# Merge products as three passes over high and low parts, with outgoing weights parted one unit ahead

## Chip, cores and metric

One core of a Trainium2 chip. The time is that of one execution on the device in microseconds. TensorE (PE) does the matrix products, VectorE (DVE), ScalarE (ACT) and GpSimd (POOL) the elementwise work, and SyncE (SP) issues most DMAs. The profile's weight loads stand under PEld.

## What is computed

A decoder trunk of two layers over 512 tokens of width 1024. Each layer normalizes x, projects it, runs four mixers and merges them with sigmoid gates; an output projection and an MLP follow:

```python
h = rms_norm(x, mix_norm_g)
p_gdn, p_mla, p_rwkv, p_dsa, gates = split(h @ w_in)   # gates: four of width 1024
y_b = mixer_b(p_b)                                     # (512, 256) for each branch b
merged = sum over b of sigmoid(gate_b) * (y_b @ w_out_b)
x = x + merged @ w_o
x = x + relu(rms_norm(x) @ w_up) ** 2 @ w_down
```

The mixers are a gated DeltaNet (GDN), multi-head latent attention (MLA), RWKV-7 and an attention over the 128 keys that an indexer selects for each query (DSA). The change touches `y_b @ w_out_b` alone.

## The kernel before

**Units.** All large weights come in one stream of 134 units a layer, a unit being 1024 rows by 128 columns, in the order of `UNITS` (L59 to 77). 32 of a layer's units are `("merge", branch, i)`: the gate weights for output columns 128i to 128i+127 and, with them, the outgoing weights `w_out` of the same columns (256 rows). The branches come in the order RWKV (2), GDN (0), MLA (1), DSA (3). In this text merges are numbered 0 to 31 in a layer: 0 to 7 RWKV, 8 to 15 GDN, 16 to 23 MLA, 24 to 31 DSA.

**Large products in parts.** A gate or projection is not an fp32 product. The weights are split into `w_hi` (an ACT copy to fp32r, L1179) and `w_lo` (what is left, a POOL subtraction in two halves, L447); the activations likewise into `h_hi` and `h_lo`. `split_product` (L480) makes 24 passes: `w_hi` by `h_hi` and by `h_lo` for eight tiles of rows, then `w_lo` by `h_hi`. `SPLIT = 2` split units exist at once; ACT makes the next one in `split_next` (L1173) when it has taken the result of the unit two before. SP loads unit g when POOL is done with unit g-3 (`RING = 3`, L409).

**Merges.** `merge` (L549) makes two gates and then two outgoing products (`merge_outputs`, L556). An outgoing product is a plain fp32 one over two tiles of 128 rows: `out_ring` (the weights, six slots) by `yo` (the mixer's output, two buffers in turn). ACT takes each gate through a sigmoid into `sg` (`merge_sig`, L1142), DVE multiplies it with the outgoing product and adds it to `mg` (`merge`, L1675) and signals `mg_done`. SP loads the outgoing weights right behind the gate weights of the same unit and waits for `mg_done` of the merge six before (L414).

**Order of the work.** Each engine runs a written-out list; an instruction that waits holds up all behind it on its engine. In a layer: RWKV's projections and scan; merges 0 to 3, whose products wait for `r_out`; GDN's preparation, merges 4 to 7, GDN's scan; DSA's projections; merges 8 to 15, between them index scores on PE (`index_pair`), ACT (`rectify_pair`) and DVE (`score_pair`), and on DVE the selection of 128 keys, dealt out in steps by `go_on` (L2002), each a MAX8 and a MATCH_REPLACE. Then MLA's attention with the gates of merges 16 to 18 made in pieces between its products, the gate of 19, and the products of 16 to 19 once `m_y` counts 8, that is once all outputs are evicted; merges 20 to 23; DSA's attention with 24 to 26 in pieces, 27, products, 28 to 31; then `wo`, `up` and `down`.

**DVE around MLA's attention** (L2069 to 2078): `attention`, `go_on(9)`, four merges, `go_on(8)`, two merges, the rest of the selection, two merges, DSA's `attention`. DVE's `attention` (L1692) takes scores from `bank_v` (L1706) and scales the exponentials (L1714, L1715). ACT's `attention` (L1213) makes the exponentials, evicts the transposes and evicts each output block of 128x128 to `yo` (L1232), the last of them three steps after its last exponential. `R["o"]` times `R["g"]` (L1887) and `G["o"]` times `G["z"]` (L1938) are the outputs of the other two mixers, written to `yo` by DVE.

## Time and profile before

| | us |
|---|---|
| median of 3 runs | 2047.19 (2046.12 to 2048.41) |
| profiled execution | 2048.0 |
| its span, first to last instruction | 2046.2 |

| engine | busy | share of the span |
|---|---|---|
| PE | 1988.9 | 97% |
| PEld | 1527.7 | 75% |
| DVE | 1090.5 | 53% |
| ACT | 768.6 | 38% |
| POOL | 737.9 | 36% |

Busy time is what lies between start and end of instructions. Each instruction's line is that of `kernel.py`; where a helper issues it (L1513 is `tt`, L1516 `ts`), tile names tell which it is. An idle time in brackets behind an instruction names what ended it. Matmul durations overlap (0.39 us each at a spacing of 0.23), so the sums of PE are read in the chain of waits, where pieces follow each other without overlap.

### The profile page before, as it was taken

The page shows a single profiled execution, that of the slowest core. Times are in us where ns is not written, and L with a number is a line of the kernel's source. Part 1 is how long each engine was busy: PE and PEld are TensorE (multiplying, and loading weights), DVE is VectorE, ACT ScalarE, POOL GpSimd, SP SyncE. Part 2 cuts the span into 40 slices and gives each one's busy share as a digit, 9 for nine tenths or more (in the row PEclk, how much of TensorE's full clock was granted, in tenths as well). Part 3 has the DMA queues.
Part 4 walks back from the last instruction along what each step waited for, and adds up shares of the span by engine and source line. Part 5 has one row for each costly group of instructions (what it writes and reads, how often), then busy time and mean ns, then how long its engine had stood idle before and what let it go on. Part 6 is the DMA issues. An engine that isn't in the chain of part 4 may idle for free.

```text
span 2046.2 us, 31754 instructions
## 1 busy us (share of the span) xinstructions
PE 1988.9 (97%) x13120; PEld 1527.7 (75%) x13120; DVE 1090.5 (53%) x1816; ACT 768.6 (38%) x1207; POOL 737.9 (36%) x551
## 2 busy tenths in 40 slices
PE   6999999999999999999999999999999999999997
PEld 4778787756667888888877877776566778888886
DVE  8785555896833422222387756379966343222223
ACT  4542523344353342322354353234344434332323
POOL 3431313422323444444445132243213344444442
PEclk9999999999999999999999999999999999999999
DMA  6220212221312333232232111123122223333232
GB/s 234 74 77 27 65 33 67 83 75 50 121 49 83 112 96 100 93 103 93 93 124 86 52 37 58 43 78 101 52 71 87 67 83 103 93 98 99 93 103 73
DMA packets 51807, 170.21 MB, mean 83 GB/s; under 512 B 5696, under 2 KB 14016, under 8 KB 51024
## 3 DMA queue, kind: packets, MB, share of 16 engines
q1 hardware_dynamic: 50448, 163.11, 24.9%
q0 software_dynamic: 1216, 5.07, 0.7%
q8 instruction: 105, 1.72, 0.3%
q14 instruction: 38, 0.31, 0.0%
HBM read 160.82 MB, written 7.34 MB: 82 GB/s over the span
## 4 chain that ended last, share of the span: by engine, by line
PE 84%; DVE 11%; ACT 3%; issue 1%; DMA 0%; POOL 0%; ACTq 0%; SPq 0%; DVEq 0%
PE bank_a L486 13%; PE bank_a L492 13%; PE bank_a L487 12%; PE bank_v L492 7%; PE bank_v L486 7%; PE bank_v L487 7%; PE bank_v L562 4%; PE bank_v L640 3%; DVE arena L1513 1%; PE bank_a L799 1%; PE bank_f L594 1%; PE bank_f L600 1%; PE bank_f L573 1%; DVE mg L1519 1%; PE bank_a L788 1%
## 5 line engine op out<-in xcount | busy, mean ns | idle before, releaser
L447 POOL TENSOR_TENSOR w_lo<-ring,w_hi 128x512 fp32r<-128x512 f32 x536 | 731.0, 1384 | 1211.6 <-ACT w_hi L1179 1211.5
L486 PE MATMUL bank_a<-h_hi,w_hi 128*128 128x512 f32 x1296 | 523.8, 404 | 3.3 <-DVE h_lo L1552 3.3
L487 PE MATMUL bank_a<-h_lo,w_hi 128*128 128x512 f32 x1296 | 505.4, 390 | 0.0
L1179 ACT ACTIVATE w_hi<-ring 128x1024 fp32r<-128x1024 f32 x268 | 281.5, 1051 | 223.7 <-DVE arena L2116 212.4
L492 PE MATMUL bank_a<-h_hi,w_lo 128*128 128x512 f32 x1296 | 321.6, 390 | 0.0
L486 PEld LDWEIGHTS bank_a<-h_hi,w_hi 128*128 128x128 f32 x1296 | 243.3, 188 | 74.5 <-issue 19.4
L487 PEld LDWEIGHTS bank_a<-h_lo,w_hi 128*128 128x128 f32 x1296 | 243.6, 188 | 57.1 <-issue 8.1
L492 PEld LDWEIGHTS bank_a<-h_hi,w_lo 128*128 128x128 f32 x1296 | 244.2, 189 | 50.9
L486 PE MATMUL bank_v<-parts,w_hi 128*128 128x512 f32 x640 | 251.3, 393 | 1.4 <-DVE parts L2085 1.4
L487 PE MATMUL bank_v<-parts,w_hi 128*128 128x512 f32 x640 | 249.1, 389 | 0.0
L1513 DVE TENSOR_TENSOR sg<-bank_v,sg 128x512 f32<-128x512 f32 x112 | 77.4, 692 | 310.4 <-PE bank_v L492 239.3
L2104 DVE TENSOR_TENSOR arena<-arena 128x512 f32<-128x512 f32 x64 | 44.3, 692 | 245.0 <-ACT arena L1472 245.0
L492 PE MATMUL bank_v<-parts,w_lo 128*128 128x512 f32 x640 | 158.1, 389 | 0.0
L486 PEld LDWEIGHTS bank_v<-parts,w_hi 128*128 128x128 f32 x640 | 120.2, 188 | 29.0 <-DVE parts L2085 4.1
L492 PEld LDWEIGHTS bank_v<-parts,w_lo 128*128 128x128 f32 x640 | 120.2, 188 | 25.0
L487 PEld LDWEIGHTS bank_v<-parts,w_hi 128*128 128x128 f32 x640 | 120.2, 188 | 24.9 <-issue 0.5
L1472 ACT ACTIVATE arena<-bank_a 128x512 f32<-128x512 f32 x64 | 38.3, 598 | 205.6 <-PE bank_a L492 205.6
L562 PE MATMUL bank_v<-yo,out_ring 128*128 128x512 f32 x256 | 114.7, 594 | 0.0
L1149 ACT ACTIVATE sg<-bank_a 128x512 f32<-128x512 f32 x52 | 31.1, 597 | 202.1 <-PE bank_a L492 202.0
L1513 DVE TENSOR_TENSOR arena<-arena 128x512 f32<-128x512 f32 (+3 forms) x78 | 98.5, 1263 | 10.7 <-ACT arena L1242 8.2
L562 PEld LDWEIGHTS bank_v<-yo,out_ring 128*128 128x128 f32 x256 | 48.0, 189 | 54.5 <-issue 53.0
L640 PE MATMUL bank_v<-arena 64*64 64x64 f32 x2176 | 65.6, 219 | 2.3 <-ACT arena L1102 2.1
(295 smaller groups left out, 2509.8 us busy)
## 6 DMA issues: line engine op xcount, KB each, us to landing
ring<-in_w SPq DMA_DIRECT2D x268, 512.0 KB, 3.5
out_ring<-in_w SPq DMA_DIRECT2D x64, 128.0 KB, 3.4
x_dram<-arena SPq DMA_DIRECT2D x2, 2048.0 KB, 8.2
arena<-x_dram SPq DMA_DIRECT2D x2, 2048.0 KB, 9.4
arena<-in_x SPq DMA_DIRECT2D x2, 1024.0 KB, 8.5
arena<-tabs POOLq DMA_DIRECT2D x4, 512.0 KB, 4.8
out_x<-arena SPq DMA_DIRECT2D x4, 512.0 KB, 4.0
consts<-in_const SPq DMA_DIRECT2D x1, 1189.0 KB, 13.3
```

The costliest lines, as they stand in the source:

```text
L447: ins = nc.gpsimd.tensor_tensor(w_lo[:, g % SPLIT, ks, :], raw, w_hi[:, g % SPLIT, ks, :].bitcast(F32), ALU.subtract)
L486: mm(b[:], w_hi[:, s, k, :], hi[:, k, :], start=k == 0, stop=False)
L487: mm(b[:], w_hi[:, s, k, :], lo[:, k, :], start=False, stop=False)
L492: ins = mm(b[:], w_lo[:, s, k, :], hi[:, k, :], start=False, stop=k == KT - 1)
L562: ins = mm(b[:], out_ring[:, n % OUT_RING, k, :], yo[:, slot, k, :], start=k == 0, stop=k == 1)
L573: mm(b[:], hi[:, k, :], h_hi[:, k, :], start=k == 0, stop=False)
L640: ins = mm(b[quarter(p_), k * C:(k + 1) * C], lhs[quarter(p_), m, :], rhs(m, p_), start=True, stop=True)
L1149: act_fn(sg[:, n % GATES, :], b[:], ACT.Sigmoid).then_inc(S["mg_sig"], 1)
L1179: act_fn(w_hi[:, g % SPLIT, :, :], ring[:, g % RING, :, :], ACT.Copy).then_inc(S["split_hi"], 1)
L1472: act_fn(relu[:, n % 2, :], b[:], ACT.Relu).then_inc(S["up_relu"], 1)
L1513: link(v.tensor_tensor(out_, a, b, op))
L2104: v.tensor_tensor(relu2[:, n % 2, :], relu[:, n % 2, :], relu[:, n % 2, :], MUL).then_inc(S["up_sq"], 1)
```

## The change

The outgoing product becomes six fp32r passes in place of two fp32 matmuls. For this
- the outgoing weights are parted: `out_hi` by ACT in `split_next`, ahead of the gate weights of the following unit; `out_lo` by POOL, ahead of that unit's `w_lo`. SP loads them behind the following unit's gate weights. `out_ring` lies over `out_lo`, and the slots go from six to four;
- the mixer outputs are parted: RWKV's and GDN's by DVE in `parts_of` (a copy and a subtraction for each of two tiles of 128x512), those of the attentions by ACT, which evicts each block twice (`y_hi` and a plain copy `yt`), and by DVE, which subtracts in `low_rows` once for each 128 queries, the last time at the end of `attention`;
- one pair `y_hi`, `y_lo` takes the place of the two buffers of `yo`; PE waits for the new events `r_yl`, `g_yl`, `m_yl`, `d_yl` and `ow_lo`.

```diff
-OUT_RING = 6
+OUT_RING = 4
@@ SP
-                if UNITS[u][0] == "merge":
-                    n = merges_to(g)
+                if g and UNITS[(g - 1) % NU][0] == "merge":
+                    n = merges_to(g - 1)
                     if n >= OUT_RING:
                         sp.wait_ge(S["mg_done"], n - OUT_RING + 1)
-                    sp.dma_start(out_ring[:, n % OUT_RING, :, :], wstream[g, :, KT * P:].rearrange("p (k n) -> p k n", n=P)).then_inc(out_here[n % OUT_RING], 16)
+                    sp.dma_start(out_ring[:, n % OUT_RING, :, :], wstream[g - 1, :, KT * P:].rearrange("p (k n) -> p k n", n=P)).then_inc(out_here[n % OUT_RING], 16)
@@ POOL
+                if g and UNITS[(g - 1) % NU][0] == "merge":
+                    n = merges_to(g - 1)
+                    pool.wait_ge(S["ow_hi"], n + 1)
+                    slot = n % OUT_RING
+                    nc.gpsimd.tensor_tensor(out_lo[:, slot, :, :], out_ring[:, slot, :, :], out_hi[:, slot, :, :].bitcast(F32), ALU.subtract).then_inc(S["ow_lo"], 1)
@@ PE, merge_outputs
-                    pe.wait_ge(out_here[n % OUT_RING], 16 * (n // OUT_RING + 1))
+                    pe.wait_ge(S["ow_lo"], n + 1)
+                    hi, lo = out_hi[:, n % OUT_RING], out_lo[:, n % OUT_RING]
                     for k in range(2):
-                        ins = mm(b[:], out_ring[:, n % OUT_RING, k, :], yo[:, slot, k, :], start=k == 0, stop=k == 1)
+                        mm(b[:], hi[:, k, :], y_hi[:, k, :], start=k == 0, stop=False)
+                        mm(b[:], hi[:, k, :], y_lo[:, k, :], start=False, stop=False)
+                    for k in range(2):
+                        ins = mm(b[:], lo[:, k, :], y_hi[:, k, :], start=False, stop=k == 1)
@@ ACT, split_next
+                if g and g < L * NU and UNITS[(g - 1) % NU][0] == "merge":
+                    n = merges_to(g - 1)
+                    if n >= OUT_RING:
+                        act.wait_ge(S["mg_done"], n - OUT_RING + 1)
+                    act.wait_ge(out_here[n % OUT_RING], 16 * (n // OUT_RING + 1))
+                    act_fn(out_hi[:, n % OUT_RING, :, :], out_ring[:, n % OUT_RING, :, :], ACT.Copy).then_inc(S["ow_hi"], 1)
@@ ACT, attention
-                        act_fn(yo[:, slot, h // 2, qt * P:(qt + 1) * P], b[:, 0:P], ACT.Copy).then_inc(S[x + "_y"], 1)
+                        rows = slice(qt * P, (qt + 1) * P)
+                        act_fn(y_hi[:, h // 2, rows], b[:, 0:P], ACT.Copy)
+                        act_fn(V["yt"][:, h // 2, rows], b[:, 0:P], ACT.Copy).then_inc(S[x + "_y"], 1)
@@ DVE
+            def parts_of(l, x, src):
+
+                for f in range(2):
+                    link(v.tensor_copy(y_hi[:, f, :], src[:, f, :]))
+                    v.tensor_tensor(y_lo[:, f, :], src[:, f, :], y_hi[:, f, :].bitcast(F32), SUB).then_inc(S[x + "_yl"], 1)
+
+            def low_rows(l, x, V, qt):
+
+                rows = slice(qt * P, (qt + 1) * P)
+                dve.wait_ge(S[x + "_y"], at(l, x + "_y", 2 * qt + 2))
+                v.tensor_tensor(y_lo[:, :, rows], V["yt"][:, :, rows], y_hi[:, :, rows].bitcast(F32), SUB).then_inc(S[x + "_yl"], 1)
+
@@ DVE, attention
+                    if i >= 8 and i % 4 == 0:
+                        low_rows(l, x, V, i // 4 - 2)
+                low_rows(l, x, V, TT - 1)
@@ DVE, mixer outputs
-                v.tensor_tensor(yo[:, 0, :, :], R["o"], R["g"], MUL).then_inc(S["r_out"], 1)
+                v.tensor_tensor(R["o"], R["o"], R["g"], MUL).then_inc(S["r_out"], 1)
                 dve.wait_ge(S["r_out"], reached("r_out"))
+                parts_of(l, "r", R["o"])
```

## Rows read from the trace of the kernel before

**Rows 1.** Page: busy us (share) xinstructions; chain that ended last, by engine.
```profile
PE 1988.9 (97%) x13120; PEld 1527.7 (75%) x13120; DVE 1090.5 (53%) x1816; ACT 768.6 (38%) x1207; POOL 737.9 (36%) x551
...
PE 84%; DVE 11%; ACT 3%; issue 1%; DMA 0%; POOL 0%; ACTq 0%; SPq 0%; DVEq 0%
```

**Rows 2.** Busy time by stage: stretch, length, PE, PEld, DVE, ACT, POOL, clock, DMA.
```profile
374.30:475.00 100.70, 100.21 (x372) 62.48 (x370) 95.03 (x168) 39.37 (x59) 31.91 (x23) 1.00 0.22 71
...
512.80:555.80 43.00, 42.76 (x160) 29.37 (x160) 39.22 (x66) 13.68 (x18) 16.36 (x12) 1.00 0.37 128
...
591.70:635.50 43.80, 43.12 (x163) 29.97 (x161) 15.99 (x22) 17.44 (x25) 16.52 (x12) 1.00 0.22 68
```

**Rows 3.** Time order of DVE in E: start, us, instruction, idle before.
```profile
399.87 2.87 DVE L1969 SCALAR_TENSOR_TENSOR arena<-arena,ab 128x384 f32<-128x384 f32 x2 [0.26 <-ACT arena L1391]
...
417.48 0.43 DVE L1513 TENSOR_TENSOR arena<-arena 128x256 f32<-128x256 f32 x1
...
432.48 3.03 DVE L1969 SCALAR_TENSOR_TENSOR arena<-arena,ab 128x512 f32<-128x512 f32 x2 [0.41 <-ACT arena L1391]
```

**Rows 4.** Time order of PE at the start of F.
```profile
475.14 0.46 PE L779 MATMUL bank_v<-arena 96*128 96x128 f32 x2 [0.63 <-DVE mg L1688]
```

**Rows 5.** Time order of DVE in G.
```profile
506.67 0.49 DVE L1715 TENSOR_SCALAR arena<-arena,att 128x512 f32<-128x512 f32 x1
...
521.50 1.62 DVE L1688 TENSOR_TENSOR mg<-mg,sg 128x512 f32<-128x512 f32 x1
...
552.38 0.69 DVE L1513 TENSOR_TENSOR sg<-bank_v,sg 128x512 f32<-128x512 f32 x1 [2.01 <-PE bank_v L562]
...
555.77 0.29 DVE L1706 CUSTOM_DVE_ANT_0 arena<-bank_v,consts 128x128 f32<-128x128 f32 x1
```

**Rows 6.** Time order of DVE in layer 1's G.
```profile
1555.70 0.69 DVE L1513 TENSOR_TENSOR sg<-bank_v,sg 128x512 f32<-128x512 f32 x1 [2.01 <-PE bank_v L562]
```

**Rows 7.** Chain that ended last, in time order: start, us, what.
```profile
220.73 1.81 PE bank_a L492 x8
...
222.54 6.87 PE bank_v L562 x16
...
1053.07 3.03 PE bank_a L492 x8
```

**Rows 8.** Time order of ACT in A.
```profile
205.04 1.05 ACT L1179 ACTIVATE w_hi<-ring 128x1024 fp32r<-128x1024 f32 x1
...
224.14 1.28 ACT L1359 ACT_TABLE_LOAD   x1
```

**Rows 9.** Time order of ACT at the end of F.
```profile
512.80 0.28 ACT L1232 ACTIVATE yo<-bank_a 128x128 f32<-128x128 f32 x1 [2.29 <-PE bank_a L799]
```

**Rows 10.** Time order of PE in A.
```profile
215.95 1.12 PE L765 MATMUL bank_a<-arena,consts 128*128 128x512 f32 x2 [1.66 <-ACT arena L1240]
```

**Rows 11.** Time order of DVE in A.
```profile
214.82 2.17 DVE L1887 TENSOR_TENSOR yo<-arena 128x1024 f32<-128x1024 f32 x1
...
224.35 0.69 DVE L1684 TENSOR_TENSOR mg<-bank_v,sg 128x512 f32<-128x512 f32 x1 [4.92 <-PE bank_v L562]
```

**Rows 12.** Loads of outgoing weights (L415), from issue to landing.
```profile
DMA to landing us min/median/max: 2.0/3.4/5.8
```

**Rows 13.** Waits: who waited for whom, us in total, times, longest.
```profile
DVE arena L1513 <- PE bank_v L965: 21.3, 12, 2.1
```

**Rows 14.** By line: xcount, duration in ns, min/median/max.
```profile
L2012 DVE TENSOR_TENSOR arena<-arena x16: 691/1659/1670, 336.6 to 1379.9; 128x512 f32<-128x512 f32 x16
...
L447 POOL TENSOR_TENSOR w_lo<-ring,w_hi x536: 1257/1288/3221, 19.5 to 2026.0; 128x512 fp32r<-128x512 f32 x179
...
L1983 DVE MATCH_REPLACE8 arena<-m,arena x90: 407/542/678, 380.4 to 1542.3; 128x256 f32<-128x256 f32 x30, 128x384 f32<-128x384 f32 x30, 128x512 f32<-128x512 f32 x30
```

**Rows 15.** Busy time and granted clock (the value before the DMA share), layer 1.
```profile
1053.00:1056.00 3.00, 3.00 (x10) 2.33 (x9) 2.83 (x6) 0.00 (x0) 0.00 (x0) 0.58 0.35 139
```

**Rows 16.** Time order of SP's queue in G.
```profile
523.15 0.33 SPq L415 DMA_DIRECT2D out_ring<-in_w  x1
```

More of the change, by code:

```diff
@@ L44 @@
 BLOCK = 8
-INVERSE_STEPS = ("uc", "e", "x1", "ti", "y", "t", "x", "wt", "u")
+INVERSE_STEPS = ("yl", "uc", "e", "x1", "ti", "y", "t", "x", "wt", "u")
 GDN0, MLA0, RWK0, DSA0, GATE0 = 0, 1032, 1448, 2472, 3824
@@ L181, in build @@
         ring = sb("ring", [P, RING, KT, P])
-        out_ring = sb("out_ring", [P, OUT_RING, 2, P])
+        out_hi = sb("out_hi", [P, OUT_RING, 2, P], F32R)
+        with nc.sbuf_tensor("out_ring", [P, OUT_RING, 2, P], F32) as out_ring:
+            pass
+        out_lo = sb("out_lo", [P, OUT_RING, 2, P], F32R)
         w_hi = sb("w_hi", [P, SPLIT, KT, P], F32R)
@@ L186, in build @@
         par = sb("par", [P, NPAR])
-        yo = sb("yo", [P, 2, 2, T])
+        y_hi = sb("y_hi", [P, 2, T], F32R)
+        y_lo = sb("y_lo", [P, 2, T], F32R)
         misc = sb("misc", [P, 2, T])
@@ L285, in build @@
             ("m_ss", 16), ("m_p", 16), ("m_n", 16), ("m_pt", 16), ("m_y", 8),
+            ("r_yl", 2), ("g_yl", 2), ("m_yl", 4), ("d_yl", 4), ("ow_hi", 32), ("ow_lo", 32),
             ("mg_sig", 32), ("mg_raw", 6), ("mg_done", 32), ("mg_hi", 8), ("mg_lo", 8), ("wo_done", 8), ("up_relu", 32), ("up_sq", 32), ("up_hi", 32), ("up_done", 32), ("g_zs", 1), ("r_s0", 1), ("g_s0", 1), ("down_done", 8 * QUARTERS),
@@ L373, in build @@
             iq=ar(15, (4, T)), q=ar(19, (2, T)), k=ar(21, (2, T)), vf=ar(23, (2, T)), v=ar(25, (TT, 256)), tab=ar(27, (2, T)), ik=ar(29, (T,)),
-            tmp=ar(35, (T,)), ss=ar(11, (4, T)), pt=ar(15, (4, TT, P)),
+            tmp=ar(35, (T,)), ss=ar(11, (4, T)), pt=ar(15, (4, TT, P)), yt=ar(27, (2, T)),
         )
@@ L378, in build @@
             tab=ar(27, (2, T)), tmp=ar(29, (T,)), bias=ar(32, (T,)), kr=ar(33, (T,)),
-            ss=ar(15, (4, T)), pt=ar(33, (4, TT, P)),
+            ss=ar(15, (4, T)), pt=ar(33, (4, TT, P)), yt=ar(27, (2, T)),
         )
@@ L906, in _ @@
                 more.append(gate(l, 2, 3))
-                pe.wait_ge(S["r_out"], at(l, "r_out", 1))
+                pe.wait_ge(S["r_yl"], at(l, "r_yl", 2))
                 merge_outputs(0, numbers)
@@ L984, in indexed_merge @@
                         index_pair()
+                    pe.wait_ge(S["g_yl"], at(l, "g_yl", 2))
                     merge_outputs(1, numbers)
@@ L1038, in _ @@
                 numbers.append(gate(l, 1, 3))
-                pe.wait_ge(S["m_y"], at(l, "m_y", 8))
+                pe.wait_ge(S["m_yl"], at(l, "m_yl", 4))
                 merge_outputs(0, numbers)
@@ L1049, in _ @@
                 numbers.append(gate(l, 3, 3))
-                pe.wait_ge(S["d_y"], at(l, "d_y", 8))
+                pe.wait_ge(S["d_yl"], at(l, "d_yl", 4))
                 merge_outputs(1, numbers)
@@ L1211, in norm_root, with attention @@
                         act_fn(h_hi[:, k, :], mg[:, k, :], ACT.Copy).then_inc(S["n_hi"], 1)
-            def attention(l, x, V, slot, fill):
+            def attention(l, x, V, fill):
                 steps = [(qt, h) for qt in range(TT) for h in range(H)]
@@ L1439, in _ @@
                 merge_sig(l)
-                attention(l, "m", Mv, 0, lambda i: piecewise_sig(l, i))
+                attention(l, "m", Mv, lambda i: piecewise_sig(l, i))
                 late_sig(l, 3)
@@ L1444, in _ @@
                 merge_sig(l)
-                attention(l, "d", Dv, 1, lambda i: piecewise_sig(l, i))
+                attention(l, "d", Dv, lambda i: piecewise_sig(l, i))
                 late_sig(l, 6)
@@ L1937, in _ @@
                 stt(G["o"], G["o"], pr("gdn_g", 0), G["sq2"], MUL, MUL)
-                v.tensor_tensor(yo[:, 1, :, :], G["o"], G["z"], MUL).then_inc(S["g_out"], 1)
+                v.tensor_tensor(G["o"], G["o"], G["z"], MUL).then_inc(S["g_out"], 1)
                 dve.wait_ge(S["g_out"], reached("g_out"))
+                parts_of(l, "g", G["o"])
                 dve.wait_ge(tab_d_here, 16 * (l + 1))
```

## The prediction

> **What bounds the kernel now.** I read the page first, then the busy time by stage, then the chain of waits, and last the time order of DVE, ACT, SP and POOL around the merges. The page shows a TensorE kernel: PE is busy 97% of the span and holds 84% of the chain, DVE 11% [rows 1]. So PE time taken out should come off the end, but only where PE is what others wait for. The table by stage says where that holds [rows 2]. I name stages per layer: A (195 to 235 us, first four merges), B (to 273, four more), E (374 to 475, eight merges among the index scores), F (475 to 513, MLA attention), G (513 to 556, eight merges), H (to 592, DSA attention), I (to 636, eight merges); after that come `wo`, `up` and `down` without merges. In E and G, PE is full, but DVE is nearly full too: 95.0 of 100.7 us and 39.2 of 43.0. In time order DVE in E works through from 374 on, with three idle bits for ACT's output, the first 0.26 and the last 0.41 us, 0.9 in all [rows 3]; at 475 PE waits 0.63 us for DVE's merge, not the other way [rows 4]. In G DVE goes from its last softmax scaling (506.67) through selection and merges without a gap until 550.38, idles 2.01 us, merges, and starts the next attention at 555.77 [rows 5]. So E and G have two bounds that lie within about 2 us of each other. Layer 1 repeats it 1003.3 us later, with the same 2.01 us [rows 6]. From here I work for one layer and double.
>
> **The product itself.** Four fp32 products of merges, of two matmuls each, take 6.87 us, so 1.717 each; eight passes on split operands take 1.81 us, so 0.2267 each [rows 7]. Six of those are 1.360 us. Gain 0.357 us a merge, 11.4 us a layer, 22.9 us in all, if nothing else moved. The Trainium skill, "TensorE: Matmul & The Clock Gate", section "Back-to-back issue gap", gives about 216 ns for 512 columns; its estimate would be 64 x (1.717 - 1.294) = 27 us. The rows show 227 ns here, and I go by them.
>
> **Stage A.** Gain 4 x 0.357 = 1.43. But ACT now splits the outgoing weights (128x256) ahead of each unit's. No row has this shape from SBUF; 128x1024 takes 1.05 and 128x128 from PSUM 0.28 [rows 8, 9], so it costs between 0.28 and about 0.4; I take 0.35. Two of them fall into a stretch from 204.55 on in which ACT does not idle and at whose end PE waits 1.66 us for its eviction [rows 8, 10]: +0.7. Then, after the gate at 222.5, ACT has to wait for merge 0 to be done and for the fifth outgoing weight to land, since with four slots SP's load waits for merge n-4: product 1.4 + DVE 0.7 + landing 3.4 (2.0 to 5.8) + both splits 1.3 + a table load 1.28 put the first `g_feat` eviction near 231.3, where PE wants its fourth bank about 0.55 earlier [rows 8, 11, 12]. Together A is -0.2 (-1.4 to +1.2). The splitting of R's output by DVE (two copies of at most the 0.69 of a 128x512 operation, two subtractions of 0.69, some 2.8 us) follows 216.99 and ends near 219.8, before PE comes at 222.5: free [rows 7, 11].
>
> **Stage B.** -1.4. G's output split (+2.8 on DVE at 332) is taken in by DVE's idle ahead of the rotations, 12 waits of together 21.3 us in both layers [rows 13].
>
> **Stage E.** PE's 2.86 us buy nothing: DVE sets the time. PE will instead wait at the fifth rotation product (L1028), whose bank DVE frees only near 457.6, and its lead of some 3 us ends there. DVE can lose its idle bits, -0.85. Against it stands POOL: the same 128x512 DVE operation (L2012) takes 0.69 at its shortest and 1.66 in the median, the long ones beside POOL's subtractions: +0.97 under a POOL instruction of 1.29 to 1.49 [rows 14]. POOL gets eight more (128x256, about half of 1.288, 0.65 us). At 0.97/1.49 and with two thirds of them over operations that suffer, 8 x 0.65 x 0.65 x 0.65 = +2.2 (0 to 8 x 0.65 = 5.2). MATCH_REPLACE does not suffer, its 0.678 for 512 columns is its longest [rows 14]. The Trainium skill, "SBUF — State Buffer", section "SBUF: two separate sides", says that whoever has the port pair that POOL and DVE share blocks the other for its full instruction; by that the term would be up to +5.2. The row shows about two thirds. And PE's wait of some 3 us may drop its clock: in layer 1, right after pauses of PE, a stretch shows a granted clock of 0.58, mostly the lower of the levels 1.2 and 2.4 GHz, and eight passes took 3.03 instead of 1.81 [rows 7, 15]. That is 1.2, up to 1.7 with the passes next to them; I put +1.0 (0 to 1.7). E: +2.3 (-0.9 to +6.0).
>
> **Stages F and H.** Each attention output is evicted twice, `y_hi` and the plain copy (0.28 more of ACT), twice an attention right ahead of the copy that frees PE's only `bank_f`; with three splits more, +0.5 each (0 to 1) [rows 9].
>
> **Stage G, the largest term.** `low_rows(3)` stands at the end of DVE's attention, ahead of `go_on(9)`, and waits for the last attention output. That eviction starts at 512.80 [rows 9], while DVE is done at 507.16 [rows 5]. With the second eviction, `m_y` comes near 513.25; the subtraction of 128x256 takes 0.43 [rows 3], so `go_on(9)` starts at 513.76 and not 507.07. Queued behind are 13.7 us of selection, the four merges, 12.2 us more, two merges, 7.8 us, two merges, then the scores of the next attention, all on one engine. 6.7 us late less the 2.01 of slack is +4.7. One long POOL collision (L1688 at 1.62 instead of 0.69) moves away, others come: I take +4.2 (+2.5 to +5.5). PE's 2.86 us are lost here too. Behind the same delay, SP may load outgoing weight 20 only when merge 16 is done, now near 528.9 (in the old kernel, with six slots, SP waits here for the same merge with the load of weight 22, until 523.15) [rows 16]; landing 3.4, splits 1.3, so PE's gate 21, wanted at 529.3, starts at 533.6. PE then reaches the last pair's product near 554 to 556, DVE near 556: covered, by 0 to 2 us.
>
> **Stage I.** PE leads and DVE is busy for 16.0 of 43.8 us [rows 2]. Seven of eight products count: -2.5. The wait for merge 24 here has 3 us of cover.
>
> **Sum.** A -0.2, B -1.4, E +2.3, F and H +1.0, G +4.2, I -2.5: +3.4 a layer, +6.8 in all. The profiled execution of before took 2048.0 us (span 2046.2), 0.8 above the median of 2047.2, so 2054.8 for such a one and 2054.0 for the median.
>
> **The rivals.**
> First: PE becomes the path in G. If outgoing weight 20 lands after the longest 5.8 us instead of 3.4, and the stall of 4 to 7 us lowers the clock (1.7 us), the last pair's product comes near 558.1, DVE's 556 plus 2.1, and a start of the attention at the low clock adds 1.2: 3.3 a layer, 2054.0 + 2 x 3.3 = 2060.6. For it: the cover is at most 2 us. Against: the median landing.
> Second, on the other side: POOL's runs move off DVE's vulnerable operations. POOL follows ACT, ACT follows PE, and PE is now ahead of DVE in E, so the runs may fall on MAX8 and MATCH_REPLACE, which keep their time under POOL [rows 14]. POOL is busy for 31.9 us of E [rows 2]; by the same two factors it adds 31.9 x 0.65 x 0.65 = 13 us to DVE. If 6 of these go, E shrinks to PE's own bound, -2.9, and G loses a collision of 0.9 [rows 5]. Per layer -0.2 -1.4 -2.9 +1.0 +3.3 -2.5 = -2.7: 2041.8. With under 2 us gone the forecast stands. Against: L1969 and the rotations are most of what DVE does when a unit is split.
> Third: my reading of DVE as the bound is wrong and PE's gain comes through whole: 2047.2 - 22.9 = 2024.3. The 2.01 us and the 0.63 us speak against it.
> Fourth: the six passes do not run at 0.227 each, because each product is short and loads its own weights, and take the old 1.717. Then A, B and I lose 5.3 us a layer: 2064.6. Against: the gates use the same sequence.
>
> **How the numbers follow.** Forecast 0.55, first rival 0.20, second 0.12, third 0.08, fourth 0.05. The ends of the terms sum to -3.7 and +10.8 a layer, 2039.8 and 2068.8 in all, and seldom come together; with the first two rivals inside I take 2040 to 2067. About 0.2% (4.1 us) is what a measurement can tell from no change: below 2043.1 is faster, above 2051.3 slower. Faster: the second and third rival less a little, 0.19. Slower: most of the forecast (0.38), the first and the fourth, 0.63. Same: 0.18.
>
> **What would show it.** In the profile after: the merge products at 1.36 us each; DVE idle about 6 us right after its last softmax scaling, released by ACT's attention output; no 2.01 us idle before the last pair; PE idle between the two attentions, most at gate 21 behind ACT's split and DMA; the eight DVE merges in E no earlier; stage I shorter by 2.5. I am wrong if DVE still has slack before the second attention, or if E shrinks by more than 2 us.

## The result, and the profile after

Slower, by more than predicted. The changed kernel took 2069.71 us in the median (2069.32 to 2070.10, four runs), the kernel before 2047.20 beside it: a ratio of 1.0108, with an interval of 1.0096 to 1.0120. The prediction was 2054.0 with a range of 2040 to 2067. On another chip, later, the changed kernel took 2068.04 (2067.04 to 2069.46; 1.0096, 1.0082 to 1.0110; run e8 below). The profiled execution took 2070.1, its span is 2068.3.

From the page of the changed kernel: busy time, shares of the chain, POOL's new group, and the landing of the outgoing weights.

```profile
PE 1987.1 (96%) x13248; PEld 1562.0 (76%) x13248; DVE 1124.2 (54%) x1848; ACT 793.3 (38%) x1303; POOL 797.0 (39%) x615
...
PE 77%; DVE 18%; ACT 3%; issue 2%; DMA 0%; POOL 0%; ACTq 0%; SPq 0%; DVEq 0%
...
L452 POOL TENSOR_TENSOR out_lo<-out_ring,out_hi 128x256 fp32r<-128x256 f32 x64 | 55.2, 862 | 404.1 <-ACT out_hi L1197 404.1
...
out_ring<-in_w SPq DMA_DIRECT2D x64, 128.0 KB, 3.4
```

DVE's share of the chain went from 11% to 18% [rows 1]: more of the span hangs on DVE than before.

The product did what was computed for it. Two products of stage A in time order on PE:

```profile
227.76 0.39 PE L573 MATMUL bank_v<-y_hi,out_hi 128*128 128x512 f32 x1
...
228.69 0.63 PE L576 MATMUL bank_v<-y_hi,out_lo 128*128 128x512 f32 x2
229.16 0.40 PE L573 MATMUL bank_v<-y_hi,out_hi 128*128 128x512 f32 x1
```

229.16 - 227.76 = 1.40 us a product, where 1.717 was the price before [rows 7] and 1.360 the forecast.

Then stage by stage. I compared the two traces at marks that both have: ACT's splits of the gate weights, and the first and last score that DVE takes in each attention (L1741 after, L1706 before). The time of a mark in the changed kernel less that of the same mark in the kernel before is an offset; a stage's loss is the growth of the offset over it, in us. The first row ends at the split of unit 12 (99 us), so the second holds RWKV's scan besides A and B; finer marks follow under e12.

| stage | predicted | after, layer 0 | layer 1 | e8, layer 0 | layer 1 |
|---|---|---|---|---|---|
| start, up to unit 12 | 0 | +2.45 | +0.26 | -0.15 | +0.23 |
| unit 12 to 28, with A and B | -1.6 | -1.03 | +0.19 | -1.89 | +0.10 |
| E | +2.3 | +0.36 | +0.36 | +0.37 | +0.35 |
| F | +0.5 | +1.97 | +1.74 | +2.21 | +1.85 |
| G | +4.2 | +6.99 | +6.89 | +7.09 | +6.95 |
| H | +0.5 | +3.19 | +3.19 | +3.24 | +3.20 |
| I | -2.5 | -2.25 | -2.22 | -2.24 | -2.23 |
| sum | +3.4 | +11.7 | +10.4 | +8.6 | +10.4 |

G, F and H carry it. DVE in G of the changed kernel, in time order (start, duration, idle time ahead of it and what ended that):

```profile
476.82 0.29 DVE L1741 CUSTOM_DVE_ANT_0 arena<-bank_v,arena 128x128 f32<-128x128 f32 x1
...
507.71 0.68 DVE L1741 CUSTOM_DVE_ANT_0 arena<-bank_v,arena 128x512 f32<-128x512 f32 x1
...
510.29 0.48 DVE L1750 TENSOR_SCALAR arena<-arena,att 128x512 f32<-128x512 f32 x1
510.69 0.42 DVE L1725 TENSOR_TENSOR y_lo<-arena,y_hi 128x256 fp32r<-128x256 f32 x1
516.74 0.43 DVE L1725 TENSOR_TENSOR y_lo<-arena,y_hi 128x256 fp32r<-128x256 f32 x1 [5.63 <-ACT arena L1255]
517.08 0.41 DVE L1539 TENSOR_SCALAR arena<-arena,m 128x384 f32<-128x384 f32 x1
...
538.10 1.78 DVE L1711 TENSOR_TENSOR mg<-mg,sg 128x512 f32<-128x512 f32 x1
...
557.76 2.19 DVE L2032 TENSOR_TENSOR_SCAN arena<-arena 128x512 f32<-128x512 f32 x1
...
566.52 0.29 DVE L1741 CUSTOM_DVE_ANT_0 arena<-bank_v,consts 128x128 f32<-128x128 f32 x1
```

The reader is to see three things. DVE idles 5.63 us for the last attention output before `go_on(9)`; from 517.08 to 566.52 it has no gap, so the 2.01 us before the last pair [rows 5] are gone; and the stretch from the first operation of the selection to the next attention is 566.52 - 517.08 = 49.44 us long, where before it was 555.77 - 507.07 = 48.70 with those 2.01 in it, 46.69 of work. So the same operations take 2.75 us longer. Paired one by one, 75 in either trace, they do so beside POOL: of those that changed by over 0.05 us every one that grew now runs beside a POOL instruction and did not before (the addition at 538.10 from 0.69 to 1.78, the scan at 557.76 from 1.23 to 2.19), and every one that shrank lost all or part of such an overlap.

PE around the pauses of the same trace:

```profile
458.78 1.10 PE L1043 MATMUL bank_v<-arena,consts 96*96 96x512 f32 x2 [1.15 <-DVE arena L2094]
...
476.94 0.46 PE L793 MATMUL bank_v<-arena 96*128 96x128 f32 x2 [1.75 <-DVE mg L1711]
...
538.03 0.80 PE L496 MATMUL bank_a<-h_hi,w_hi 128*128 128x512 f32 x1 [5.09 <-ACT w_hi L1200]
...
541.18 0.63 PE L497 MATMUL bank_a<-h_lo,w_hi 128*128 128x512 f32 x1
541.61 0.63 PE L496 MATMUL bank_a<-h_hi,w_hi 128*128 128x512 f32 x1
...
566.63 0.55 PE L793 MATMUL bank_v<-arena 64*128 64x128 f32 x1 [2.66 <-DVE mg L1711]
```

The pause of 1.15 us lies at the rotation product in E. The one of 5.09 us is gate 21, which stands behind ACT's wait for outgoing weight 20:

```profile
516.26 0.28 ACT L1254 ACTIVATE y_hi<-bank_a 128x128 fp32r<-128x128 f32 x1 [2.28 <-PE bank_a L813]
...
536.61 0.42 ACT L1197 ACTIVATE out_hi<-out_ring 128x256 fp32r<-128x256 f32 x1 [14.10 <-DMA out_ring<-in_w]
```

Behind gate 21's pause the passes come 0.43 us apart (541.18, 541.61) instead of 0.23. The table by stretch shows the lower clock there and behind the two pauses at the attentions; behind the one at 458.78 the clock stayed up (behind the window stand its length, the busy time of PE, PEld, DVE, ACT and POOL, then the granted clock, 1.00 being the full one, and DMA's share and rate):

```profile
17.00:31.00 14.00, 8.62 (x25) 6.36 (x26) 10.08 (x13) 9.32 (x18) 6.17 (x4) 0.51 0.36 118
218.00:222.00 4.00, 3.74 (x7) 2.30 (x8) 3.90 (x5) 3.03 (x5) 2.54 (x2) 0.57 0.00 0
478.00:482.00 4.00, 3.68 (x12) 2.97 (x13) 1.35 (x9) 1.41 (x7) 0.00 (x0) 0.60 0.36 130
536.00:543.00 7.00, 4.97 (x12) 3.92 (x13) 6.73 (x11) 3.21 (x5) 5.77 (x6) 0.53 0.71 216
567.00:574.00 7.00, 6.41 (x22) 4.08 (x21) 2.35 (x16) 2.36 (x11) 0.00 (x0) 0.55 0.24 83
```

At the start, in stage A, at the start of the MLA attention, at gate 21 and at the start of the DSA attention PE runs at the lower of its two levels, 1.2 instead of 2.4 GHz, for 3.4 us or twice that (more at the start). The kernel before shows the lower level in one stretch only, from 1052 to 1055 [rows 15], and in its last microseconds.

### The profile page after: what moved, and what is told of

It reads as the page before. It is cut to its first block, busy times and chain, and to the rows that moved or that the text cites. A ratio compares the mean times of both kernels' runs of the same rounds, so it can differ in the third digit from the quotient of the medians.

```text
span 2068.3 us, 32262 instructions
## 1 busy us (share of the span) xinstructions
PE 1987.1 (96%) x13248; PEld 1562.0 (76%) x13248; DVE 1124.2 (54%) x1848; ACT 793.3 (38%) x1303; POOL 797.0 (39%) x615
## 3 DMA queue, kind: packets, MB, share of 16 engines
q8 instruction: 106, 1.74, 0.3%
## 4 chain that ended last, share of the span: by engine, by line
PE 77%; DVE 18%; ACT 3%; issue 2%; DMA 0%; POOL 0%; ACTq 0%; SPq 0%; DVEq 0%
PE bank_a L502 11%; PE bank_a L496 11%; PE bank_a L497 11%; PE bank_v L502 7%; PE bank_v L496 7%; PE bank_v L497 7%; PE bank_v L654 3%; DVE arena L2023 2%; DVE m L2021 2%; DVE arena L1536 2%; DVE mg L1711 1%; PE bank_f L608 1%; DVE sg L1536 1%; PE bank_f L609 1%; PE bank_a L813 1%
## 5 line engine op out<-in xcount | busy, mean ns | idle before, releaser
L1200 ACT ACTIVATE w_hi<-ring 128x1024 fp32r<-128x1024 f32 x268 | 281.7, 1051 | 224.5 <-DVE arena L2156 212.4
L452 POOL TENSOR_TENSOR out_lo<-out_ring,out_hi 128x256 fp32r<-128x256 f32 x64 | 55.2, 862 | 404.1 <-ACT out_hi L1197 404.1
L654 PEld LDWEIGHTS bank_v<-arena 64*64 64x64 f32 x2176 | 64.5, 135 | 3.1 <-ACT arena L1117 2.8
## 6 DMA issues: line engine op xcount, KB each, us to landing
consts<-in_const SPq DMA_DIRECT2D x1, 1189.0 KB, 13.7
```

The source lines that it names most:

```text
L452: nc.gpsimd.tensor_tensor(out_lo[:, slot, :, :], out_ring[:, slot, :, :], out_hi[:, slot, :, :].bitcast(F32), ALU.subtract).then_inc(S["ow ...
L654: ins = mm(b[quarter(p_), k * C:(k + 1) * C], lhs[quarter(p_), m, :], rhs(m, p_), start=True, stop=True)
L1200: act_fn(w_hi[:, g % SPLIT, :, :], ring[:, g % RING, :, :], ACT.Copy).then_inc(S["split_hi"], 1)
```

## The experiments

After the first result the theory was: DVE sets G; its wait is most of what G lost; and PE's pauses ahead of the attentions cost once more, through the clock. The rivals: gate 21's late weights set G; F and H are longer for ACT's second eviction; POOL's new instructions slow DVE down.

### e1: the wait alone, in the kernel before

```diff
                 attention(l, "m", Mv, 96 ** -0.5, lambda qt: Mv["bias"][:, (3 - qt) * P:T])
+                dve.wait_ge(S["m_y"], at(l, "m_y", 8))
                 go_on(9)
```

> The kernel before, with one wait added: DVE waits for the last MLA attention output ahead of the selection in stage G, as the changed kernel does; no operation is added, the products stay fp32. Theory (that wait is most of what G lost, and DVE is G's bound): the selection starts near 513.3 instead of 507.07, 6.2 later, less the 2.01 of slack: +4.2 a layer, so 2047.2 + 8.4 = 2055.6; if PE's longer pause ahead of the second attention also lowers its clock, up to +1.5 a layer more, 2058.6. Rival (the loss in G comes from the outgoing weights that arrive late at gate 21, not from DVE's wait): no change, 2047.2 within 1.

Measured: 2062.76 us, ratio 1.0071 (1.0054 to 1.0088), 14 us for one wait (the profiled execution was a short one, its span 2057.4). The first line is DVE's, the second PE's at the second attention:

```profile
511.93 0.42 DVE L1516 TENSOR_SCALAR arena<-arena,m 128x384 f32<-128x384 f32 x1 [5.96 <-ACT yo L1232]
```

```profile
560.08 0.55 PE L779 MATMUL bank_v<-arena 64*128 64x128 f32 x1 [5.71 <-DVE mg L1688]
```

By the marks G grew by 5.38 us in layer 0 and 5.35 in layer 1: the selection started 6.04 later against the offset it came with, less the slack of 2.01, plus 1.35 by which DVE's operations got longer (511.93 to 559.97 is 48.04, against 46.69 of work), though none was added. H grew by 1.06 and 1.92, with the lower clock from 557 to 564 and from 1567 to 1574. G and H of both layers together are 13.7 of the 14 us. The rival with no change falls. Above the forecast of 4.2 for G are the 1.35: moving DVE's work by 6 us against POOL's made it longer without any POOL instruction more. Here too each operation that grew did so beside POOL.

### e2, e3, e4: each wait taken away alone, and both

e2 subtracts the last low part three selection steps later:

```diff
-                low_rows(l, x, V, TT - 1)
...
-                go_on(9)
+                go_on(3)
+                low_rows(l, "m", Mv, TT - 1)
+                go_on(6)
```

(for the DSA attention it stays at the end). e3 changes the order of the splits on ACT, and on POOL alike:

```diff
-                    act_fn(out_hi[:, n % OUT_RING, :, :], out_ring[:, n % OUT_RING, :, :], ACT.Copy).then_inc(S["ow_hi"], 1)
...
                     act_fn(w_hi[:, g % SPLIT, :, :], ring[:, g % RING, :, :],
                            ACT.Copy).then_inc(S["split_hi"], 1)
...
+                    act_fn(out_hi[:, n % OUT_RING, :, :], out_ring[:, n % OUT_RING, :, :], ACT.Copy).then_inc(S["ow_hi"], 1)
```

(the two waits ahead of the moved line move with it). 
e4 has both.

> The changed kernel, with the last low part of the MLA attention output subtracted three selection steps later, so that DVE doesn't wait for ACT ahead of the selection. Theory (DVE bound, PE close behind): DVE's chain in G comes 6 us earlier, but PE's last pair of products, 2.5 us ahead of DVE in the trace of after, then sets the end; so 2.5 a layer is won, and up to 1.5 more if PE's pause ahead of the second attention and its low clock go: 2069.7 - 5.0 = 2064.7, down to 2061.7. Rival one (the gate blocked by the outgoing weights is what sets G): no change, 2069.7. Rival two (DVE alone, PE has room): the full 6.4 a layer, 2056.9.

> The changed kernel, with ACT and POOL splitting each unit's own weights ahead of the outgoing weights of the unit before, so that gate 21 doesn't stand behind the load of outgoing weight 20. Theory (DVE bound): PE's wait of 5.09 us at gate 21 goes, but the stage ends no earlier, since DVE works without a gap from 516.7 to 566.5; PE waits longer ahead of the second attention instead; 2069.7 within 2. Rival one (gate 21's block sets G): 4 to 5 us a layer less, near 2061. Rival two (the order costs in stages A and I, where PE leads, since w_hi comes earlier but the product's own weights later): 1 to 2 us either way.

> The changed kernel with both edits: the last low part later and each unit's own weights split first. Theory: only both together give G back, since after either one the other engine sets the end: 6.4 us a layer, 2056.9, and with the low clock at the start of the second attention gone (up to 2 a layer) 2053. Rival one (either one alone gives it all): the same time as the better of the two single edits. Rival two (the extra work on DVE and the collisions with POOL hold G up too, whatever PE does): 3 us a layer less than after, 2063.

Measured: e2 2052.76 us, 1.0023 (1.0014 to 1.0032); e3 2062.73, 1.0068 (1.0053 to 1.0084); e4 2048.73, 1.0000 (0.9991 to 1.0010). The kernel before took 2048.52 in these runs.

e2 gave far more than I expected: G's loss fell from 7.0 to 0.90 and -0.06. My expectation had PE held at gate 21 as before. But gate 21 waits for merge 16, merge 16 for DVE, and DVE was late by the same wait. With DVE 6 us earlier the split of unit 51 came 8 us earlier (offset 9.9 instead of 18.0; 1.3 of the 8 were there when G began) and PE had no pause there. DVE's wait, now among the selection steps, is 1.22 us; PE's pause ahead of the attention stays:

```profile
515.48 0.43 DVE L1725 TENSOR_TENSOR y_lo<-arena,y_hi 128x256 fp32r<-128x256 f32 x1 [1.22 <-ACT arena L1255]
```

```profile
559.21 0.51 PE L793 MATMUL bank_v<-arena 64*128 64x128 f32 x1 [4.10 <-DVE mg L1711]
```

e3 took the pause at gate 21 away, and G still lost 6.36 and 6.02 us. PE's time went into two other pauses, one for POOL's low part of outgoing weight 20, one for DVE:

```profile
540.41 0.77 PE L573 MATMUL bank_v<-y_hi,out_hi 128*128 128x512 f32 x1 [3.91 <-POOL out_lo L458]
...
562.41 0.55 PE L793 MATMUL bank_v<-arena 64*128 64x128 f32 x1 [3.63 <-DVE mg L1711]
```

What e3 won (5.3 us against e8's 2068.04) was mostly outside G: E gave 0.3 instead of losing 0.36; F lost only 0.35 in layer 0, where the clock stayed up after a pause of 1.28 us instead of 1.75, and H 2.04 and 2.24.

So of the 19.3 us between e8's time and e4's most are DVE's wait: 15.3 when it goes first (e8 to e2), 14.0 when it goes last (e3 to e4). In e4 G is shorter than before, by 0.67 and 0.69, and F costs 0.35 at the full clock; H still lost 1.9 and 1.8.

### e5, e9, e10: PE kept busy in its pauses

The passes added are ones whose result is overwritten by the product that follows in the same bank; `spare` is the bank of the first transpose, taken a little earlier:

```diff
+            def keep_busy(b, g, count):
+                for k in range(count):
+                    mm(b[:], w_hi[:, g % SPLIT, k % KT, :], h_hi[:, k % KT, :], start=True, stop=True)
...
+                    if i == 2:
+                        spare, reader, emptied = banks.next("a", x + "_pt")
+                        pe.wait_ge(reader, emptied)
+                        g = unit[0] - 1
+                        keep_busy(spare, g, FILL[x][0])
```

(and `FILL[x][1]` passes behind the scores that follow).

> The kernel of e4 (last low part later, own weights split first), plus passes of 128x512 on PE whose result is thrown away, where PE waits for DVE at the start of each attention: 5 and 2 at the MLA one (its two waits there are 1.28 and 0.70 us), 9 and 3 at the DSA one (2.22 and 0.89 us); 0.2267 us each. Theory (PE's pauses let its clock fall to the lower level, and that costs time in the 3.4 or 6.8 us after them): with the pauses filled the clock stays at its upper level through both attentions; the 1.9 and 1.8 us that the DSA attention lost in the two layers of e4 come back, and 1.6 in layer 1's MLA attention; from the 2048.7 of e4 to 2044.5 (2043 to 2046). Rival one (the attentions are longer because of the second eviction on ACT, the clock is only a companion): 2048.7 within 1. Rival two (the added passes come on the path): 19 x 0.2267 x 2 = 8.6 more, 2057.

Measured: 2043.11 us, 0.9977 (0.9967 to 0.9987): 5 us less than e4 by 38 passes more. The stretch after the start of the second attention, in e4 and then in e5:

```profile
556.00:562.00 6.00, 5.11 (x20) 3.32 (x21) 2.19 (x15) 2.25 (x10) 0.00 (x0) 0.72 0.31 105
```

```profile
556.00:564.00 8.00, 7.84 (x40) 4.83 (x40) 4.39 (x23) 4.13 (x18) 0.00 (x0) 1.00 0.31 98
```

H lost 0.27 and 0.29 instead of 1.9 and 1.8, F in layer 1 0.11 instead of 1.58.

e9 does the same to the changed kernel, in its own order.

> The changed kernel in its own order (neither wait moved), with thrown-away passes of 128x512 in PE's pauses at the start of the attentions: 7 and 3 at the MLA one (its waits are 1.75 and 0.70 us), 11 and 2 at the DSA one (2.66 and 0.59), 0.2267 us each, 5.2 us more PE work a layer. Theory (the clock that falls after these pauses is 1.5 us of stage F's loss and 2.9 of H's): both attentions keep the upper level, F falls from +2.0 to +0.4 and H from +3.2 to +0.4 against the kernel before, 4.4 a layer, 2068.5 - 8.8 = 2059.7 (2058 to 2062). Rival (F and H are longer for the second eviction and the three splits, not for the clock): 2068.5 within 1.5, or above it where the passes are too many.

Measured: 2059.15 us, 1.0052 (1.0036 to 1.0067), 9 below e8. Stage F and H by windows, e8 first, then e9:

```profile
473.40:512.30 38.90, 36.72 (x208) 25.82 (x210) 17.36 (x67) 21.88 (x68) 6.52 (x6) 0.96 0.10 31
563.40:600.00 36.60, 34.39 (x196) 21.84 (x197) 17.02 (x67) 21.82 (x68) 6.53 (x6) 0.91 0.10 34
```

```profile
474.70:512.30 37.60, 36.03 (x215) 25.29 (x217) 17.42 (x68) 21.88 (x68) 6.52 (x6) 1.00 0.11 32
563.70:600.00 36.30, 34.53 (x219) 22.02 (x219) 17.02 (x67) 21.88 (x68) 6.52 (x6) 1.00 0.11 34
```

F lost 0.61 and 0.43 (2.21 and 1.85 without the passes), H 0.70 and 0.72 (3.24 and 3.20); G stayed at 7.62 and 7.06. ACT's second evictions and splits are all still there, so the clock was 1.5 of F's loss and 2.5 of H's. The rival of e9, that F and H are longer for ACT's work, keeps the 0.4 to 0.7 that is left.

e10 adds eight passes in PE's wait in stage A.

```diff
                 for i in range(tiles):
+                    if i == 3:
+                        pe.wait_ge(S["g_z"], at(l, "g_z", 2))
+                        for k in range(KT):
+                            mm(bank_f[0][:], h_hi[:, k, 0:P], h_hi[:, k, :], start=True, stop=True)
```

> The kernel of e5 with eight more thrown-away passes in the one pause that still lowered the clock there, PE's wait of 2.12 us for ACT at the fourth sum of squares in stage A (low from 216 to 220 and from 1220 to 1224). Theory: those two stretches go, 1.7 us each at most, less the 0.3 by which the passes may come late: from 2043.1 to 2040.5 (2039.5 to 2042). Rival one (there DVE or ACT sets the pace, and a faster PE only waits): 2043.1 within 1. Rival two (the passes come on the path): 2043.1 + 3.6 = 2046.7.

Measured: 2043.53 us, 0.9974 (0.9964 to 0.9985), against 0.9977 of e5: no difference that the runs can tell. The two low stretches did go, and by the marks A and B together gave -1.13 and +0.08, in e5 +1.05 and +2.13; but its profiled execution had the lower clock at the start (17 to 31 and 51 to 54) and from 1051 to 1054, which e5's had not. The trace is for the theory, the median doesn't confirm it. A reason is on record: four of e5's nine executions took 2041.6 to 2042.1 us at a mean granted clock of 0.998, higher than the 0.996 of its trace (2045.7), so the two low stretches of stage A were hardly in them. What the trace of e10 shows beside that: even at the full clock A and B gave less than the -1.89 of e8; the table under e12 has the reason.

### e6 and e11: without POOL's subtraction

```diff
-                    pool.wait_ge(S["ow_hi"], n + 1)
-                    slot = n % OUT_RING
-                    nc.gpsimd.tensor_tensor(out_lo[:, slot, :, :], out_ring[:, slot, :, :], out_hi[:, slot, :, :].bitcast(F32), ALU.subtract).then_inc(S["ow_lo"], 1)
...
-                    pe.wait_ge(S["ow_lo"], n + 1)
-                    hi, lo = out_hi[:, n % OUT_RING], out_lo[:, n % OUT_RING]
+                    pe.wait_ge(S["ow_hi"], n + 1)
+                    hi, lo = out_hi[:, n % OUT_RING], out_hi[:, n % OUT_RING]
```

e6 has it on e4, e11 on the changed kernel.

> The kernel of e4 without POOL's subtraction for the outgoing weights: the last two passes of each product read the high part once more (so the outputs lack the weights' low part), PE does as many passes as before, POOL 32 instructions less a layer. Theory (POOL's instructions slow DVE's down beside them, and DVE is the bound of E and G): by the prediction's own factors 16 x 0.75 x 0.65 x 0.65 = 5.1 us less DVE time a layer; PE, 1 to 2 us behind in both stages, lets 1 to 3 of them through: 2048.7 - 4 = 2044.7 (2042 to 2047). Rival one (the collisions only move from one operation to another and sum to nothing): 2048.7 within 1. Rival two: PE's products wait for POOL's low part somewhere on the path, then up to 1 us for each of the four stages more comes off, 2040.

> The changed kernel in its own order without POOL's subtraction for the outgoing weights; the last two passes of each product read the high part once more, so the outputs lack the weights' low part. It asks what POOL's 32 instructions a layer cost in stage E (mis-sized in the prediction, +2.3, measured +0.37 from the fourth unit of E to the attention) and in G (+2.75 of longer DVE operations). Theory: E gets to -0.85, the idle bits that PE's lead gives back, so POOL costs 1.2 there, half of what was predicted; G's DVE operations get 1 to 2.5 shorter, and the attention starts that much earlier; two layers: 3 to 7 us off 2068.5, 2061.5 to 2065.5. Rival (they only move): E +0.37 and G +7.0 stay.

Measured: e6 2041.67 us, 0.9968 (0.9956 to 0.9980); e11 2063.46 in its one time. In e11 E went from +0.36 to -0.06 and -0.05, so POOL's eight instructions cost 0.4 us there, and G's stretch from the selection's first operation to the next attention took 48.50 us (515.47 to 563.97) instead of 49.44 (in layer 1 48.69 instead of 49.35), so they cost 0.9 and 0.7 in G. In e6 the same stretch took 46.48 against e4's 47.52, and E 0.35 less. POOL's price is real and near 1.3 us a layer in E and G, not the 5.1 of my expectation. Another 0.3 to 0.5 goes between the splits of units 12 and 18, ahead of A: whether later work takes it in isn't shown.

The rest of e6's gain over e4 is not POOL's price on DVE. In B e6 gave 1.29 and 1.51 us (from PE's first pass on unit 23 to that on unit 27), where e4 gave nothing (+0.16 and -0.01). There e4 has a pause that e6 hasn't, PE waiting for POOL's low part:

```profile
251.21 0.47 PE L573 MATMUL bank_v<-y_hi,out_hi 128*128 128x512 f32 x1 [1.21 <-POOL out_lo L458]
```

So rival two of e6 holds for B. The changed kernel, with the outgoing weights first, has no such pause, and B gave 1.3 and 1.5 in it as in e11. Beside that the clock stayed up in H of e6's layer 1, and H lost 0.34.

```profile
515.47 0.41 DVE L1534 TENSOR_SCALAR arena<-arena,m 128x384 f32<-128x384 f32 x1
...
563.97 0.29 DVE L1736 CUSTOM_DVE_ANT_0 arena<-bank_v,consts 128x128 f32<-128x128 f32 x1
```

### e7: where PE's time counts

```diff
                     for k in range(2):
+                        mm(b[:], lo[:, k, :], y_lo[:, k, :], start=False, stop=False)
                         ins = mm(b[:], lo[:, k, :], y_hi[:, k, :], start=False, stop=k == 1)
```

> The kernel of e4 with eight passes instead of six in each product of a merge (the low part of the weights also meets the low part of the output), 8 x 0.2267 = 1.81 us a product, 0.45 more than six and 0.1 more than the fp32 product of the kernel before. Theory (PE's time counts in stages A, B and I, and DVE sets E and G): 15 to 16 of 32 products a layer count, 16 x 0.455 = 7.3, less what shorter pauses give back through the clock, up to 2: 2048.7 + 13 = 2061.5 (2057 to 2064). Rival one (PE sets the time in every stage): 64 x 0.455 = 29, 2078. Rival two (DVE sets it everywhere): 2048.7.

Measured: 2062.60 us, 1.0070 (1.0056 to 1.0083), 13.9 above e4. By the marks, against e4: A and B +3.2 and +2.8 (eight products more by 0.455 would be 3.6), E +1.6 and +1.6, G +1.6 and +1.6, I +2.8 and +2.8, H -1.5 and -1.5, for with longer products PE hardly paused there and its clock stayed up. So E and G hide 2.0 of the 3.6 us of PE each and pass the rest on; the theory had them hide it all.

### e8: the changed kernel again

> The changed kernel once more, unchanged, on the chip of these runs. In its first trace the clock was at the lower level from 17.4 to 31.1 us after the start, which by unit 8 had cost 2.4 us; the kernels e1, e3 and e4 ran the same start at the full clock, e2 not. Theory one (the start has no part in the change, and whether the clock falls there varies between executions): its times spread over 2 us or more, and this trace may show a full clock there. Theory two (it belongs to this kernel): the low stretch is there again and the times agree within 1 us. On either the rest of the losses, 4.8 a layer in G and H besides A, stands as in the first trace: 2066 to 2071.

Measured: 2068.04 us (2067.04 to 2069.46), 1.0096. Its start ran at the full clock:

```profile
17.00:31.00 14.00, 8.73 (x31) 6.23 (x30) 10.77 (x14) 9.27 (x17) 6.19 (x4) 1.00 0.39 134
```

The low start was in the profiled executions of e2, e7, e10, e11 and e12 too, and not in those of e1, e3 to e6 and e9. No operation of the change lies there. The times of the kernel before point to the same in it: of 55 executions beside these experiments 28 had a mean granted clock of 0.994 or less and a median of 2049.2 us, 23 one of 0.996 or more and 2046.8, and 17 us at the lower level (the start and 51 to 54) would take 0.004 off the mean, an estimate from the traces. So the 2.4 us are hardly part of the change, though the one trace of the kernel before has no low start. E, F, G, H and I repeat within 0.3 us.

### e12: the fastest

e10 with each unit's own weights first only after gates of E, F and G:

```diff
+def own_first(g):
+    return UNITS[(g - 1) % NU][0:2] in (("merge", 0), ("merge", 1))
```

> The kernel of e10 with one difference: each unit's own weights are split first only after gates of stages E, F and G; in A, B, H and I the outgoing weights come first again, as in the changed kernel. Theory (own weights first costs in A and B, since there the products want the outgoing low part soon: stages A and B together gave -1.9 in the changed kernel at the full clock and -1.2 and +0.1 in e10): A and B give 1.9 a layer again, G and H stay as in e10, 0.7 to 2.0 a layer off: from 2043.5 to 2041 (2039.5 to 2042.5), the fastest of all. Rival (the difference in A and B was the clock and the phase of the start, not the order): 2043.5 within 1.

Measured: 2041.03 us, 0.9972 (0.9961 to 0.9983); e10 had 0.9974. A and B gave -2.67 and -1.11 us, where e10 had -1.13 and +0.08, as the theory has it; against that G was shorter than before by 0.22 and 0.23 (0.68 and 0.69 in e10), and H lost 0.7 instead of 0.3. The ratios of the two overlap, so the order of the splits is shown by the marks and not by the times. That it beats the kernel before, by 0.28% (0.17 to 0.39), is shown.

The first pass of PE on a unit is a finer mark. It parts the row of A and B in each trace (layer 0, layer 1; growth of the offset in us; "low": PE's lower clock from about 217 to 221 or 1225 to 1235):

| run | split first | unit 12 to 19 (106 to 199 us), with RWKV's scan | 19 to 23 (to 237), A | 23 to 27 (to 306), B |
|---|---|---|---|---|
| e1 (nothing changed here) | | -1.10, -0.22 | +0.02, +0.01 | -0.04, -0.01 |
| after | outgoing | -0.75, +0.65 | +1.05 low, +1.01 low | -1.33, -1.47 |
| e8 | outgoing | +0.07, +0.55 | -0.63, +1.05 low | -1.33, -1.51 |
| e2 | outgoing | -0.31, +0.73 | -0.60, +1.01 low | -1.31, -1.49 |
| e12 | outgoing | -0.75, +0.67 | -0.59, -0.30 | -1.33, -1.51 |
| e4 | own | -0.68, +0.91 | +1.03 low, -0.63 | +0.16, -0.01 |
| e10 | own | -0.71, +0.73 | -0.59, -0.63 | +0.15, -0.03 |

The lower clock in A costs 1.65 us each time. To split a unit's own weights first costs 1.5 us in B and nothing in A. And the stretch with RWKV's scan differs by more than 1 us between traces of the same layer.

## Why the prediction was wrong

The direction was right, and so was the main reason: DVE sets E and G, and of PE's gain of 11.4 us a layer only the part in A, B and I comes through. The sum was +3.4 a layer and came out at 8.8 to 10.2 without the start. Two steps failed. In G the term for DVE's collisions with POOL was put at -0.5 and measured +2.75. In F, H and A the lower clock behind PE's pauses was put at nothing, and it measured 1.5, 2.5 and 1.6 us. A third, E at +2.3 against +0.36, failed the other way and hid part of it. Point by point:

- **The product.** 1.360 forecast, 1.40 measured (1.40 to 1.50 over all that follow each other). The fourth rival (no faster than 1.717) is out, and so is the third (the whole gain); of the second, that E shrinks, nothing is seen.
- **A and B, -1.6.** Near where PE's clock stayed up: -0.6 in A and -1.3 in B (layer 0 of e8 and e2), against -0.2 and -1.4. Where it fell behind PE's wait for ACT, A lost 1.0. That wait grew from 1.66 us [rows 10] to 2.12 by ACT's two splits, 0.46 and not 0.7; it was counted, what the clock makes of it was not. The other wait in A, of 0.55 for the first `g_feat` eviction, isn't in the trace: from 200 to 275 PE has the pause of 2.12 and no other above 0.1 (and the pieces given for it add up to 230.6, not 231.3). POOL's subtraction takes 0.86 us in the mean, not 0.65, and ACT's split 0.41, not 0.35.
- **E, +2.3.** Measured +0.36. Three terms, each off: the idle bits of 0.85 didn't go (DVE's idle time in E is 1.1 us in both kernels, since they end with ACT's output and not with PE's); the collisions cost 0.4 instead of 2.2 (e11); the clock, put at +1.0, stayed up after the pause at 458.78, of 1.15 us and not 3. The Trainium skill, "SBUF — State Buffer", section "SBUF: two separate sides", says that one of the two engines blocks the other for its whole instruction; the estimate by that was up to 5.2, and the net 0.4 of e11 is far below it, though it doesn't tell how long a single instruction blocks another. My factor was wrong in kind: it charged two thirds of the POOL instructions added, but of the eight in E four ran beside MAX8 and MATCH_REPLACE alone, which keep their time beside POOL.
- **F, +0.5.** At the full clock 0.35 (layer 0 of e3 and e4) to 0.6 (e9): right. Measured with the clock down: 1.7 to 2.2. The missing term is the clock, 1.5.
- **G, +4.2.** The step was right in kind. DVE's wait delays the selection by 6.25 us against the marks (forecast 6.7), and the slack of 2.01 is used up (forecast so). Gate 21 stalls behind ACT: until 538.03, less the 3.9 by which the stage began late 534.1, where 533.6 was forecast. And e2 and e3 show that DVE's wait and not the gate is the bound, against the first rival. The term that was mis-sized is the collisions: I put -0.5, since one goes away. They are +2.75, of which POOL's new work is 0.9 (e11; 0.7 in layer 1); e1, with no new work at all, has 1.35 of it from the mere shift of DVE against POOL.
- **H, +0.5.** At the full clock 0.27 (e5) to 0.7 (e9): right. Measured 3.2, and 2.5 of it is the clock. I had written this very mechanism down, in E and in the first rival with 1.2 us, and had a row for it. I did not put it where the largest pause arises, behind G: if DVE is the bound and PE leads, PE must pause ahead of the attention, and it did, for 2.66 us.
- **I, -2.5.** Measured -2.2.
- **The range.** Its upper end took the terms one by one from rows at the full clock; F, G and H each came out above the upper end of their own term (1, 5.5 and 1). With 4.0 a layer for the clock in F and H, 1.6 for it in A, 3.2 for DVE's operations in G, -0.4 for its wait and -1.9 for E, the sum is 3.4 + 4.0 + 1.6 + 3.2 - 0.4 - 1.9 = 9.9, and 2067.0 in all; e8 took 2068.04. Its layer 0, in which the clock stayed up in A, has 8.8 without the start. The first trace had the low start besides, 2.4 us.

What stays open: why after the same pause the clock falls in one execution and not in the next, and what moves the stretch with RWKV's scan by more than 1 us between traces. And e10 against e5 and e12 against e10 are within the spread of the times. That POOL slows DVE is shown by which operations grew; which of its instructions meet which of DVE's could not be forecast from what I had.

## What to carry to other kernels

A pause on TensorE can cost twice: once as it stands, and once as a slower stretch behind it. So when an edit makes PE lead, find where it will wait, and put that wait's second price (1.5 to 2.5 us in these traces) into the range, or fill the pause with passes whose result is thrown away. When a low or high part of something is made by an engine whose order is written out, ask what that engine has queued behind the wait: moving one subtraction a layer three steps back in DVE's list gave 15 us (e8 to e2), where the faster products of both layers save PE 64 x 0.317 = 20. And a large shift of DVE against POOL changes which operations meet, even when none is added: it cost 1.35 us in e1's G. Give it a term of either sign (G's DVE operations came out between 0.7 us shorter in e4 and 3.4 longer in e9), and don't price it by the instructions added alone.

## What the runs showed of the hardware

**The clock falls after short pauses, and not always.** Pauses of 1.28 and 0.70 us close together: full clock in layer 0 of e4, lower in layer 1. A pause of 2.12 us in stage A: lower clock in layer 0 of the first trace, full in layer 0 of e2, e3 and e8. Pauses of 0.72 and 0.95 us at the start of layer 1 of the kernel before: lower from 1052 to 1055, and full behind the same pauses in e1, e2, e5 and e7, whose layer 1 had gained 1.0 to 1.1 us on the kernel before by unit 12. The pause of 1.15 to 1.20 us in E lowered it in no trace. The stretches at the lower level were 3.4 or 6.8 us long wherever they followed such a pause, and cost up to half of that: H lost 0.3 without one, 1.9 with one of 3.4 us (e4) and 3.2 with one of 6.8 us (after).

**More work, less time.** 38 passes more on PE took 5 us off (e4 to e5), 46 took 9 off (e8 to e9).

**DVE beside POOL.** The same addition of a merge (L1711, 128x512) took 0.69 us in each of 26 cases without a POOL instruction beside it, and up to 1.81 with one; at 538.10 it was 1.78. The scan (L2032) took 1.23 in the kernel before and 2.19 beside POOL. MAX8 and MATCH_REPLACE of 512 columns took 0.69 to 0.70 and 0.67 to 0.68 with or without POOL.
